# Two layers of a hybrid encoder on one core: later M2 and M5 loads, paired M6 adds, and a last tile that is closed in halves

## What is computed

```python
for l in range(2):
    h = rms_norm(x, norm_mix[l])
    proj = h @ w_in[l]                       # q, k, v, u, gate values
    att = window_attention(q, k, v, sinks[l])
    sgu = spatial_gating(gelu(u), gelu(gv), w_s[l], b_s[l])
    x = x + concatenate([att, sgu]) @ w_o[l]
    h = rms_norm(x, norm_ffn[l])
    x = x + square(relu(h @ w_up[l])) @ w_down[l]     # 1024 -> 4096 -> 1024
return rms_norm(x, norm_final)
```

## Time and profile before

| | us |
|---|---|
| median of 3 runs | 981.32 |
| lowest and highest | 976.36, 981.49 |
| the profiled execution, own time | 976.09 |
| its span, first to last instruction | 974.3 |

### The profile page before, as it was taken

How to read it: one execution, slowest core, us unless ns; L and a number is a source line. 1 busy time by engine, 2 the same in 40 slices (tenths; PEclk the granted TensorE clock), 3 DMA queues, 4 the chain that set the end, 5 groups by cost and what they waited for, 6 DMA issues and landing times.

```text
span 974.3 us, 11766 instructions
## 1 busy us (share of the span) xinstructions
PE 953.7 (98%) x4628; PEld 790.6 (81%) x4628; DVE 629.3 (65%) x820; ACT 486.4 (50%) x732; POOL 198.0 (20%) x123
## 2 busy tenths in 40 slices
PE   8999998999999999999999999999999999999995
PEld 5888888888888888888878888898888888888884
DVE  5575524579459558756858752445965785695596
ACT  5556524653454455355445563356435535544542
POOL 2554315110110010011056434231001101100100
PEclk9999999999999999999999999999999999999998
DMA  8332114785793784676243322079478566837832
GB/s 279 135 124 87 47 63 173 175 192 179 207 192 82 269 196 106 250 175 159 86 135 130 109 66 67 21 258 206 119 248 204 109 236 179 177 112 251 176 80 87
DMA packets 42647, 149.74 MB, mean 154 GB/s; under 512 B 5856, under 2 KB 5984, under 8 KB 42592
## 3 DMA queue, kind: packets, MB, share of 16 engines
q1 hardware_dynamic: 32784, 114.57, 33.7%
q0 software_dynamic: 9216, 33.56, 19.9%
q10 hardware_dynamic: 592, 0.86, 0.2%
HBM read 146.87 MB, written 2.10 MB: 153 GB/s over the span
## 4 chain that ended last, share of the span: by engine, by line
PE 91%; DVE 4%; ACT 2%; DMA 2%; issue 1%; SPq 0%; POOL 0%; DVEq 0%
PE bank L479 15%; PE bank L481 15%; PE bank L480 15%; PE bank L476 13%; PE bank L478 13%; PE bank L477 13%; DVE xt L1283 2%; DMA raw<-weights_in 2%; PE bank L681 1%; DVE wlo L1029 1%; PE bank L620 1%; ACT z L795 1%; PE bank L655 1%; PE bank L501 1%; PE bank L665 1%
## 5 line engine op out<-in xcount | busy, mean ns | idle before, releaser
L479 PE MATMUL bank<-xhi,wlo 128*128 128x512 f32 (+1 forms) x720 | 271.9, 378 | 4.1 <-DVE xlo L1023 4.1
L481 PE MATMUL bank<-xlo,whi 128*128 128x512 f32 (+1 forms) x720 | 270.1, 375 | 0.0
L480 PE MATMUL bank<-xhi,whi 128*128 128x512 f32 (+1 forms) x720 | 270.0, 375 | 0.0
L782 ACT ACTIVATE whi<-raw 128x1024 fp32r<-128x1024 f32 x172 | 180.9, 1055 | 156.4 <-PE bank L478 103.0
L450 POOL TENSOR_TENSOR wlo<-raw,whi 128x1024 fp32r<-128x1024 f32 x53 | 142.2, 2695 | 216.7 <-ACT whi L782 216.7
L476 PE MATMUL bank<-wlo,fhi 128*128 128x512 f32 x448 | 174.5, 389 | 0.0
L478 PE MATMUL bank<-whi,flo 128*128 128x512 f32 x448 | 174.3, 389 | 0.0
L477 PE MATMUL bank<-whi,fhi 128*128 128x512 f32 x448 | 174.3, 389 | 0.0
L1029 DVE TENSOR_TENSOR wlo<-raw,whi 128x1024 fp32r<-128x1024 f32 x119 | 144.2, 1223 | 38.7 <-ACT whi L782 38.6
L457 POOL DMA_DIRECT2D raw<-weights_in x64 | 55.6, 868 | 518.4 <-DMA raw<-weights_in 516.0
L479 PEld LDWEIGHTS bank<-xhi,wlo 128*128 128x128 f32 x720 | 135.5, 188 | 29.1 <-DVE xlo L1023 4.5
(11 more groups left out here) (97 smaller groups left out, 957.9 us busy)
## 6 DMA issues: line engine op xcount, KB each, us to landing
raw<-weights_in SPq DMA_DIRECT2D x172, 512.0 KB, 4.5
raw<-weights_in POOLq DMA_DIRECT2D x64, 512.0 KB, 6.3
rawx<-weights_in SPq DMA_DIRECT2D x32, 512.0 KB, 7.0
xt<-x_in SPq DMA_DIRECT2D x4, 512.0 KB, 8.0
gbc<-gains_in SPq DMA_DIRECT2D x4, 512.0 KB, 5.4
out_t<-xt SPq DMA_DIRECT2D x3, 512.0 KB, 2.6
gbc<-gains_in ACTq DMA_DIRECT2D x1, 512.0 KB, 6.7
wst<-ws_in SPq DMA_DIRECT2D x2, 256.0 KB, 6.0
```

The lines of the kernel that those rows point to most:

```text
L479: pe.matmul(o, wlo[:, s, wc], hi[:, tokens], start=first, stop=False)
L480: pe.matmul(o, whi[:, s, wc], hi[:, tokens], start=False, stop=False)
L481: return pe.matmul(o, whi[:, s, wc], lo[:, tokens], start=False, stop=last)
L782: act.activation(whi[:, n % SLOTS, :], raw_at(slot), ACT.Copy).then_inc(whi_ready, 1)
```

## The change

Four edits, and the orders that belong to them:

- SP issues the loads of M2 and M5 behind all eight up groups.
- At a layer's end DVE makes both of M6's adds first, and ACT the squares of both tiles; `close_half` becomes `close_mixer` (at the MLP's start, with `turned_high` of the last tile ahead of `high(first + 4)`) and `close_layer`. DVE's `turned_low` of a tile stands between M5's and M7's adds.
- PE's first gate product of layer 1 takes two tiles, and the third behind the second group's first two.
- After the last layer the last tile is closed in halves: its first half's squares are taken before M7's add, that sum is scaled and given to the root as its bias, the first half is multiplied by the gain on DVE early and by the reciprocal on ACT.

```diff
@@ sync
-                    for i in range(4):
+                    for i in range(KC):
                         load_up(l, q, i)
-                    for r in (M2, M5):
-                        for g in range(2):
-                            load_block(l, q, r, g)
-                    for i in range(4, KC):
-                        load_up(l, q, i)
-                    for r in (M3, M4, M6, M7):
+                    for r in (M2, M5, M3, M4, M6, M7):
                         for g in range(2):
                             load_block(l, q, r, g)
@@ tensor
-                    gate_values(l, 0, (0, 1, 2))
+                    gate_values(l, 0, (0, 1))
                     gate_values(l, 1, (0, 1))
+                    gate_values(l, 0, (2,))
                     turn(2 * l, 3)
@@ scalar: close_mixer keeps close_half's loop, and then
+                    high(first + 3)
+                    turned_high(norm, NT - 1)
+                    high(first + 4)
+                def close_layer(norm, first):
+                    squares(norm, 0)
+                    squares(norm, 1)
+                    high(first)
+                    turned_high(norm, 0)
+                    squares(norm, 2)
+                    high(first + 1)
+                    turned_high(norm, 1)
+                    high(first + 2)
+                    turned_high(norm, 2)
+                    squares(norm, 3)
+                    high(first + 3)
+                    turned_high(norm, 3)
+                    high(first + 4)
...
+            norm = NORMS - 1
+            squares(norm, 0)
+            squares(norm, 1)
+            squares(norm, 2)
+            last = order(norm)[NT - 1]
+            act.wait_ge(x_added, added_down(DEPTH - 1, QUARTERS - 1, M5, 1))
+            act.activation(z[:, 0, :], xt[:, last, 0:512], ACT.Square, accum_out=sspart[:, 0:1]).then_inc(part_summed, 1)
+            act.wait_ge(x_added, added_down(DEPTH - 1, QUARTERS - 1, M7, 1))
+            c = norm * NT + NT - 1
+            act.activation(z[:, 1, :], xt[:, last, 512:D], ACT.Square, accum_out=ss[:, c:c + 1]).then_inc(summed, 1)
+            act.wait_ge(summed, c + 1)
+            act.wait_ge(part_ready, 1)
+            act.activation(rt[:, c:c + 1], ss[:, c:c + 1], ACT.Sqrt, scale=1.0 / D, bias=sspart[:, 1:2]) \
+                .then_inc(root_ready, 1)
+            act.wait_ge(gained, 1)
+            act.wait_ge(r_ready, c + 1)
+            act.activation(xt[:, last, 0:512], xt[:, last, 0:512], ACT.Copy, scale=rr[:, c:c + 1]).then_inc(half_ready, 1)
@@ vector, layer's end
+                add_both(last, M6)
                 if l < DEPTH - 1:
+                    normed(norm, 0)
+                    normed(norm, 1)
+                    add_product(last, M5, 0)
+                    turned_low(norm, 0)
+                    add_product(last, M7, 0)
+                    normed(norm, 2)
+                    add_product(last, M5, 1)
+                    turned_low(norm, 1)
+                    add_product(last, M7, 1)
+                    turned_low(norm, 2)
+                    normed(norm, 3)
+                    turned_low(norm, 3)
@@ vector, after the last layer
+            scaled(0)
+            scaled(1)
+            add_product(last, M5, 0)
+            add_product(last, M7, 0)
+            scaled(2)
+            add_product(last, M5, 1)
+            dve.wait_ge(part_summed, 1)
+            dve.tensor_scalar(sspart[:, 1:2], sspart[:, 0:1], 1.0 / D, EPS, ALU.mult, ALU.add).then_inc(part_ready, 1)
+            t, c = order(norm)[NT - 1], norm * NT + NT - 1
+            dve.tensor_tensor(xt[:, t, 0:512], xt[:, t, 0:512], gbc[:, 0:512], ALU.mult).then_inc(gained, 1)
+            add_product(last, M7, 1)
+            close(norm, NT - 1)
+            dve.scalar_tensor_tensor(xt[:, t, 512:D], xt[:, t, 512:D], rr[:, c:c + 1], gbc[:, 512:D],
+                                     ALU.mult, ALU.mult).then_inc(out_ready, 1)
```

More of the change, by code:

```diff
@@ L258, in build @@
         root = sb("root", [P, 1])
+        sspart = sb("sspart", [P, 2])
         banks = [ctx.enter_context(nc.psum_tensor(f"bank{i}", [P, 512], F32)) for i in range(8)]
@@ L325, in build @@
         hid_lo = sem("hid_lo")
+        part_summed = sem("part_summed")
+        part_ready = sem("part_ready")
+        gained = sem("gained")
+        half_ready = sem("half_ready")
         out_ready = sem("out_ready")
@@ L436, in _ @@
             for i, t in enumerate(order(NORMS - 1)):
[L437 to L440, removed]
+                if i < NT - 1:
+                    sp.wait_ge(out_ready, i + 1)
+                    sp.dma_start(out[t], xt[:, t, :]).then_inc(out_stored, 16)
+                else:
+                    sp.wait_ge(half_ready, 1)
+                    sp.dma_start(out[t][:, 0:512], xt[:, t, 0:512]).then_inc(out_stored, 16)
+                    sp.wait_ge(out_ready, NT)
+                    sp.dma_start(out[t][:, 512:D], xt[:, t, 512:D]).then_inc(out_stored, 16)
             sp.wait_ge(out_stored, 16 * (NT + 1))
@@ L948, in _, with close_mixer @@
                     hi(wo_pos(1, g))
-                def close_half(norm, first):
+                def close_mixer(norm, first):
                     for t in range(NT):
-                        if t and norm < NORMS - 1:
+                        if t:
                             turned_high(norm, t - 1)
                         squares(norm, t)
-                        if t == 1 and first is not None:
+                        if t == 1:
                             high(first)
-                        if t == 2 and first is not None:
+                        if t == 2:
                             high(first + 1)
                             high(first + 2)
[L961 to L966, removed]
+                    high(first + 3)
[15 more added lines that the diff above has]
+                    high(first + 4)
+                close_mixer(2 * l + 1, nth(l, up_pos(0, 0)))
                 def hidden(q, i):
@@ L999, in _ @@
                 act.activation(root[:, :], eps[:, 0:1], ACT.Sqrt)
-                close_half(2 * l + 2, nth(l + 1, 0) if l < DEPTH - 1 else None)
+                if l < DEPTH - 1:
+                    close_layer(2 * l + 2, nth(l + 1, 0))
+            norm = NORMS - 1
[15 more added lines that the diff above has]
+            act.activation(xt[:, last, 0:512], xt[:, last, 0:512], ACT.Copy, scale=rr[:, c:c + 1]).then_inc(half_ready, 1)
         @block.vector
@@ L1334, in _ @@
                         low_up(q + 1, 4)
[L1336 to L1353, removed]
@@ L1354, in _ @@
-                if l < DEPTH - 1:
-                    turned_low(norm, NT - 1)
+                norm, last = 2 * l + 2, QUARTERS - 1
+                add_both(last, M6)
+                if l < DEPTH - 1:
+                    normed(norm, 0)
[10 more added lines that the diff above has]
+                    turned_low(norm, 3)
@@ new lines, in scaled @@
+            def scaled(i):
+                close(norm, i)
+                t, c = order(norm)[i], norm * NT + i
+                dve.scalar_tensor_tensor(xt[:, t, :], xt[:, t, :], rr[:, c:c + 1], gbc[:, :], ALU.mult, ALU.mult) \
+                    .then_inc(out_ready, 1)
+            scaled(0)
[5 more added lines that the diff above has]
+            dve.wait_ge(part_summed, 1)
```

## The result

| | us |
|---|---|
| changed kernel, median of 5 runs | 969.16 (968.84 to 969.32) |
| kernel before, 5 runs beside it | 980.3 (976.36 to 981.49) |
| ratio of the two | 0.9895, 95% interval 0.9876 to 0.9913 |
| changed kernel's profiled execution | own time 969.21, span 967.3 |

The kernel is 1.05% faster, 10.3 us by the ratio (8.5 to 12.2); 8.2 were forecast. The spans of the two profiled executions differ by 7.0 only (974.27 to 967.3), so two things have to be explained: where the 7.0 come from, and where the rest is.

The account below looks back on a forecast made before the run. TensorE, busy 98% of the span, was taken as the bound, so only its stops and the tail could be won: 4.4 + 2.4 + 1.45 = 8.2 us off the median 981.32 gives 973.1, range 967 to 978.5.

Parts of the forecast that it names:

- Part A: Where the MLP begins: new load and ACT order removes PE's stops, 2.9 us in layer 0 and 1.5 in layer 1, 4.4 together.
- The M2 and M5 loads' price: In all eight quarters: M2 and M5 load later, M3's first load lands 2.9 us later in quarter 1, costing nothing.
- the cover: Quarter 1: POOL's add into M3 lands near 261.5, ACT wants the sum at 266.89, leaving 5.4 us.
- The rival of a slowdown by this way: Quarters 1 to 3, both layers: M3's sum comes late, ACT and PE wait, 988 us; chance 0.03.
- Part B: End of layer 0: PE's two stops for normed tiles 1 and 2 go, 2.5 less a new 0.1, gaining 2.4 us.
- the one new stop of 0.1: PE's second part of layer 1's first gate product wants tile 1's low at 492.6, done at 492.7.
- Part C: Tail after the last matmul: new DVE and ACT order gains 1.45 us, bounds 0.5 and 1.8.
- the 2 us that the prediction set: Tail: the prediction is wrong if the last tile's half square starts later than 2 us after the last matmul ends.
- the luck of the levels: Runs of the kernel before differ by 5.1 us (976.36 to 981.49), about what a measurement can tell from no change.

Follow-up runs that it names:

- copy_first: Kernel before with one edit: at the MLP's start ACT copies tile 3's high half ahead of high(first + 4), loads in old order; 971.95 us, ratio 0.992.
- loads_only: Kernel before with the load order alone: M2 and M5 loads behind all eight up groups; 972.72 us, ratio 0.9926.
- same_kernel: Kernel before run again with no edit, to see its scatter; 979.2 us over 11 runs, ratio 0.9993.
- layer_end_only: Kernel before with only the changed end of layer 0: DVE's order and PE's split first gate product; 976.58 us, ratio 0.9968.
- tail_only: Kernel before with only the changed end of the last layer, last tile closed in halves; 977.81 us, ratio 0.9989.
- stop_filled: Kernel before with unneeded matmuls, 20 in layer 0 and 11 in layer 1, ahead of PE's wait at the MLP's start; 977.28 us, ratio 0.9979.
- without_a: Changed kernel with old load order and high(first + 4) ahead of tile 3's copy again; 974.86 us, ratio 0.9952.

## Why the prediction was right, and where it was short

**Part A.** The mechanism held in every step: the copy of tile 3 waited behind a `high` for a load behind the M2 and M5 loads, and either edit is enough (copy_first 0.992, loads_only 0.9926, both with the others 0.9895, one with the others 0.9892). The stops' slots came out as forecast, 2.95 and 1.59 against 2.9 and 1.5. But the term of 4.4 us was too small. The prediction took a stop to cost its idle time and 0.16, because in the one execution that it read the granted clock was 1.00 right behind both stops. For that execution the term is right (copy_first, 4.5); for the median it is not.

In the execution of same_kernel the clock was half of that from 171.65 to 175.04, 1.5 us more, in those of layer_end_only and tail_only in both layers, and by the mean clocks (0.993 to 0.995, against 0.997 in the execution read) the same can be expected of the other runs; this last step is argued from the means, not seen in a trace. Filling the stops took 2.1 us off (stop_filled). So A is worth 4.4 and about 2 more in the middle of before's runs. The direct measurements lie on both sides of that: giving A back costs 5.7 (without_a, with the half clock in layer 0 alone), copy_first alone wins 7.8, by an interval of 6.4 to 9.2. Its profiled execution had a short warm-up, so some of the 7.8 may be its start; the runs do not separate the two.

**The M2 and M5 loads' price.** Nothing, as forecast, and no ACT wait for a weight's transfer is left behind 11 us. But the cover is thinner than worked out. In quarter 1 POOL issued M3's first add at 255.40, ACT began on the first up group's bank at 247.94; before, 251.47 and 249.40. Against the quarter that is 5.4 us later, not 2.9 (in loads_only it was 3.0): the four `rawx` loads landed 7.5 to 9.9 us after issue in that stretch, and M3's first load 10.1. POOL and ACT there, after:

```profile
255.40 0.86 POOL L461 DMA_DIRECT2D raw<-weights_in  x1 [42.14 <-DMA raw<-weights_in]
...
265.42 1.05 ACT L787 ACTIVATE whi<-raw 128x1024 fp32r<-128x1024 f32 x1
```

The add itself landed 5.3 us after the start of its issue, at 260.7, so 4.7 us of cover are left before ACT takes the sum at 265.42. Before, it landed at 256.9 (251.47 + 5.4) and 10.0 were left. The prediction had 6.3 and 0.86 for the add; the time to landing counts from the start of the issue, so the 0.86 was counted twice, and its 5.4 us of cover were 6.3 by its own rows. The rival of a slowdown by this way did not come.

**Part B.** 2.51 us of slots by the traces against 2.4; the one new stop of 0.1 did not show. Tile 2's transposes start 3.97 us earlier than before, and 5.46 against the start of PE's first product, where 5.4 were forecast. Alone the part measured 3.1 (2.2 to 4.2).

**Part C.** 1.41 us against 1.45, and 1.1 (0.1 to 2.1) alone. The steps inside came as written, half square to half scale; the half square starts at 960.00, 1.73 us behind the last matmul's end, within the 2 us that the prediction set.

**The sum.** 2.95 + 1.59 + 2.51 + 1.41 = 8.5 us against 8.2, and about 2 for the half clock: 10.5, where 10.3 (8.5 to 12.2) were measured. The forecast thus came right by its mechanism, and was short by one cost that it did not have. The same miss can be seen from the other side: 8.2 was worked out on an execution of 976.09, one of the shortest, with a short warm-up and no half clock, and then taken off a median that held half clock. Its 5.2 us under the median was itself a sign that stood in the prediction, read there as the luck of the levels and not looked into.

Not settled: why the half clock follows some stops and not others. In the five profiles that have layer 0's stop it followed four (2.28, 2.68, 2.77 and 2.80 us idle, but not 2.73 of the earlier trace rows), and layer 1's at 1.85 and 2.06 but not at 1.33, 1.38 and 1.50. Nor is the scatter of before explained in full: among its runs of one mean clock (0.993) the times still go from 979.0 to 981.6, and without_a, with the stops back, scattered by 1.3 us only.

## What to carry to other kernels

A short stop of TensorE may cost more than its length, because matmuls behind it can run at half the clock; read the granted clock behind each stop, in more than one execution, before pricing it. Where runs scatter, profile an execution near the median, not the shortest, and ask what differs. Look for a wait at the head of an engine's queue with urgent work behind it that needs nothing of what is waited for: moving the urgent instruction ahead is as good as making the wait shorter. And in a tail that alternates between two engines, independent adds belong into the time in which one waits for the other's root.

## What was not expected of the hardware

- A wait of PE of 2.8 us was followed by matmuls at 1.2 GHz (sixteen of them, from 0.46 us behind the stop, took 0.21 us each instead of 0.12), and the same wait filled with matmuls that nobody needs was not.
- The same 20 warm-up matmuls took 10.29 to 11.82 us in the twelve profiled executions, and shift all that follows. The five runs of the changed kernel lie within 0.5 us even so.
- The four 512 KB loads of `rawx` in quarter 1, issued one behind the other, landed 7.5 to 9.9 us after their issue, and one alone in 3.3.
